# Differential attention of a two-block transformer: the values product issued one unit later than the transposes

## What is computed

```python
def diff_attention(q, k, v, lam):
    s = jnp.einsum('bqhpd,bkhpd->bhpqk', q, k).astype(jnp.float32) * (ATT_HEAD_DIM ** -0.5)
    p = jax.nn.softmax(s, axis=-1)
    a = p[:, :, 0] - lam * p[:, :, 1]
    return jnp.einsum('bhqk,bkhe->bqhe', a.astype(v.dtype), v)
```

## Time and profile before

| what | us |
|---|---|
| median of three runs | 3123.93 |
| lowest and highest | 3122.47, 3125.21 |
| the profiled execution, its device time | 3122.81 |
| span of its trace | 3121.0 |
| TensorE busy | 2692.0 (86%) |
| VectorE busy | 1351.0 (43%) |
| ScalarE busy | 483.3 (15%) |
| chain that ended last: loads of expert weights (`in_moe_w`) | 12% of the span |
| attention stage of layer 0, first S to the end of the last o | 206.69 to 255.26 |
| attention stage of layer 1, likewise | 910.53 to 944.03 |

### The profile page before, as it was taken

One profiled execution on the slowest core, in us unless ns is written; L12 is line 12 of the kernel. 1 busy time (PEld: TensorE's weight loads), 2 busy tenths in 40 slices (PEclk: granted clock), 3 DMA queues, 4 the chain that ended last, 5 costly groups with the idle time before them and its releaser, 6 DMA issues. The chain is left out here.

```text
span 3121.0 us, 45633 instructions
## 1 busy us (share of the span) xinstructions
PE 2692.0 (86%) x19942; PEld 1662.7 (53%) x19942; DVE 1351.0 (43%) x2546; ACT 483.3 (15%) x1169; POOL 39.9 (1%) x64
## 2 busy tenths in 40 slices
PE   6988999999988999987969989879979787756656
PEld 3457844446766888635543334345459686422323
DVE  1874488533472876686221101121466763100001
ACT  1023200000122001234221001010051301100000
POOL 0000000000000000001000000000000000000000
PEclk8999999999999999998979999989999898878877
DMA  8530255432342675220229999981110016799998
GB/s 341 193 135 1 92 204 216 151 145 111 130 164 73 269 287 208 81 81 1 82 107 427 427 428 427 428 337 30 43 35 29 2 72 231 299 427 427 427 428 350
DMA packets 66358, 651.35 MB, mean 209 GB/s; under 512 B 14704, under 2 KB 25584, under 8 KB 26480
## 3 DMA queue, kind: packets, MB, share of 16 engines
q1 hardware_dynamic: 66160, 648.43, 51.5%
HBM read 644.08 MB, written 4.33 MB: 208 GB/s over the span
## 5 line engine op out<-in xcount | busy, mean ns | idle before, releaser
L369 PE MATMUL ps<-HT,ring 128*128 128x256 f32 (+1 forms) x3024 | 902.7, 458 | 29.3 <-DMA ring<-in_w_in 10.9
L369 PEld LDWEIGHTS ps<-HT,ring 128*128 128x128 f32 x3024 | 573.0, 191 | 333.7 <-issue 271.0
L1952 PE MATMUL ps<-ring,arena 128*32 128x256 f32 (+1 forms) x2976 | 374.1, 506 | 105.9 <-DMA ring<-in_moe_w 103.2
L442 DVE SCALAR_TENSOR_TENSOR acc<-ring,sil,acc 128x512 f32<-128x512 f32 x616 | 411.7, 744 | 0.0
L369 PE MATMUL ps<-arena,ring 128*128 128x256 f32 (+3 forms) x1232 | 373.6, 464 | 3.2 <-PEq L644 2.0
L1952 PEld LDWEIGHTS ps<-ring,arena 128*32 128x32 f32 (+1 forms) x2976 | 141.4, 130 | 316.0 <-issue 200.3
L369 PEld LDWEIGHTS ps<-arena,ring 128*128 128x128 f32 (+2 forms) x1232 | 230.1, 188 | 139.2 <-issue 119.1
L948 DVE SCALAR_TENSOR_TENSOR XT<-ps,modcols,XT 128x256 f32<-128x256 f32 x148 | 66.6, 481 | 356.0 <-PE ps L369 228.3
L1973 PE MATMUL ps<-ring,conv 128*64 128x512 f32 x512 | 116.1, 596 | 27.7 <-DMA ring<-in_moe_w 26.9
L1973 PE MATMUL ps<-ring,arena 128*32 128x256 f32 x960 | 86.0, 520 | 61.5 <-DMA ring<-in_moe_w 61.0
L369 PE MATMUL ps<-ring,HT 128*128 128x512 f32 (+1 forms) x288 | 105.1, 523 | 0.0
(11 more groups left out here) (366 smaller groups left out, 2657.4 us busy)
## 6 DMA issues: line engine op xcount, KB each, us to landing
ring<-in_moe_w SPq DMA_DIRECT2D x186, 2048.0 KB, 25.6
ring<-in_w_mod SPq DMA_DIRECT2D x24, 2048.0 KB, 8.4
ring<-in_ada_w SPq DMA_DIRECT2D x24, 2048.0 KB, 8.3
ring<-in_w_up SPq DMA_DIRECT2D x16, 2048.0 KB, 12.3
ring<-in_w_down SPq DMA_DIRECT2D x16, 2048.0 KB, 12.6
ring<-in_w_in SPq DMA_DIRECT2D x10, 2048.0 KB, 10.3
ring<-in_od_w_in SPq DMA_DIRECT2D x6, 2048.0 KB, 25.6
arena<-in_moe_w SPq DMA_DIRECT2D x10, 1024.0 KB, 7.3
```

The costliest lines, as they stand in the source:

```text
L369: last = nc.tensor.matmul(bank_of(job, j), lhsT, rhs, start=n == 0, stop=n == len(terms) - 1)
L442: ins = nc.vector.scalar_tensor_tensor(out=acc, in0=weights[:, k, :], scalar=s, in1=acc, op0=ALU.mult, op1=ALU.add)
L1952: last = nc.tensor.matmul(K.ps[M * j:M * j + M, 2 * (e % 2) + i, 0:FW], xs[:, e // 4 % 2, e % 4, 4 * h + k, :], weights((m, e, h), k, slic ...
```

## The change

On TensorE each turn now issues T(i-3), S(i), V(i-4); on ScalarE c(i-3), e(i); on VectorE o(i-5), m(i), p(i-1). VectorE's wait for e(i-4) ahead of m(i) is gone. The loops have one turn more. The instructions themselves, their operands, their number and the buffers stay as they are. Nothing outside this function changes.

```diff
         @block.tensor
         def _(pe):
-            for i in range(U + 3):
+            for i in range(U + 4):
+                if 3 <= i <= U + 2:
+                    j = i - 3
+                    pe.wait_ge(*K.at("probs_done", 2 * (j + 1)))
+                    if j:
+                        pe.wait_ge(*K.at("probsT_done", j))
+                    for c in range(len(units[j]["v"])):
+                        last = nc.tensor.matmul(K.ps[:, 6, c * P:(c + 1) * P], E[:, j % nb, 0, c * P:(c + 1) * P], scaled_ident[:, j % 4],
+                                                start=True, stop=True)
+                    last.then_inc(*K.inc("transposed"))
                 if i < U:
...
-                if i >= 3:
-                    j = i - 3
+                if i >= 4:
+                    j = i - 4
                     u = units[j]
                     pe.wait_ge(*K.at("probsT_done", j + 1))
...
-                if 2 <= i <= U + 1:
-                    j = i - 2
-                    pe.wait_ge(*K.at("probs_done", 2 * (j + 1)))
...
-                    last.then_inc(*K.inc("transposed"))
         @block.scalar
         def _(act):
-            for i in range(U + 2):
+            for i in range(U + 3):
+                if i >= 3:
+                    j = i - 3
+                    act.wait_ge(*K.at("transposed", j + 1))
+                    if j >= 2:
+                        act.wait_ge(*K.at("values_done", j - 1))
+                    n = P * len(units[j]["v"])
+                    nc.scalar.activation(AT[:, j % 2].rearrange("p k q -> p (k q)")[:, 0:n], K.ps[:, 6, 0:n], ACT.Copy).then_inc(*K.inc("probsT_done"))
                 if i < U:
...
-                if i >= 2:
-                    j = i - 2
-                    act.wait_ge(*K.at("transposed", j + 1))
...
         @block.vector
         def _(dve):
-            for i in range(U + 4):
-                if i >= 4:
-                    j = i - 4
+            for i in range(U + 5):
+                if i >= 5:
+                    j = i - 5
                     dve.wait_ge(*K.at("values_done", j + 1))
                     nc.vector.tensor_copy(units[j]["out"], K.ps[:, 7, 0:P]).then_inc(*K.inc("out_kept"))
                 if i < U:
                     n = units[i]["k"].shape[-1]
                     dve.wait_ge(*K.at("scores_done", i + 1))
-                    if i >= 4:
-                        dve.wait_ge(*K.at("exps_done", 2 * (i - 3)))
```

## The result

The changed kernel takes 3119.53 us (median of 22 runs, 3115.42 to 3123.84) against 3123.69 us before (22 runs, 3118.36 to 3129.64). The ratio is 0.9985, 95% interval 0.9979 to 0.9991: by it the change is worth 4.7 us, between 2.8 and 6.6 (the two medians are 4.2 apart). That is less than the 0.2% that was called no change, and it lies clear of zero. Forecast were 5.2 us and 3118.7.

What follows compares the result with a forecast made beforehand. The prediction took the two-unit chain S, m, e, c, V, T, with V waiting for c, to bound the wide units. Layer 0's 3.07 us and layer 1's 2.12 sum to 5.2 saved, giving 3118.7 us, range 3115.0 to 3123.5.

Steps and rivals of the forecast that it cites:

- The new bound of wide units: Wide units, steady state: TensorE alone, S to V to T to S, 3.04 us per unit in place of 3.23.
- The chain that bounds a head of layer 0: Layer 0, S9 to S11 over m, p, o, V6 and T8: 5.55 us of a 10.32 us head.
- the gain is passed on: After both attention stages: what they save is saved in full; the rival, not passed on, 3123.9 us, chance 0.08.
- The hand-over from o to V: VectorE to TensorE: o itself 0.28 us and 0.05 to hand over, 0.33 together.
- the tail of layer 0: Layer 0, S15 to the end of the last o: 7.96 us after, 8.24 before, 0.28 less.
- The tail of layer 1: Layer 1, S7 to the end of the last o: 10.99 us after, 11.45 before, 0.46 less.
- Layer 1: Second attention stage: start 0.89, S4 to S7 0.77 and tail 0.46, together 2.12 us saved.
- the chain through ScalarE: Wide units: S, m, e, c, V, T closes over three units, 6.46 / 3 = 2.15 us each, and drops out.
- the first rival: Layer 0: TensorE alone bounds it, a head takes 9.54 us; 7.3 us saved, 3116.6 us; chance 0.16.
- The wait for o: Slower rival: V(i-4) waits on `out_kept`, two-unit chain 7.31 us if o comes behind one p more; about 3132 us; chance 0.03.
- the 0.3 per head that was named as a sign: Layer 0: V's idle wait for o, expected at about 0.3 us per head if the forecast holds.
- The clock rival: Low-clock stretch on TensorE more or less, 1.7 us either way: 3117.0 or 3120.4 us; chance 0.13.

Runs made afterwards that it cites:

- the one kernel above that does not fit: Changed kernel with V(i-5), o(i-6) and room for three units in AT: 3119.45 us, ratio 0.9981 to the kernel before.
- the first pair of traces: First traced execution of the kernel before and of the changed kernel: layer 0 48.54 and 46.09 us, layer 1 33.47 and 30.80.
- the second traces on both sides: Kernel before and changed kernel traced again without edit: layer 0 48.54 and 47.15 us, layer 1 31.53 and 29.74.
- the two repeats: Changed kernel run twice more without edit: 3120.19 and 3120.55 us, ratios 0.9990 and 0.9991 to the kernel before.

## Why the prediction was right, and where not

**What held.** Order, not work: T keeps its place among the S's, ScalarE's list is unchanged, and only V moves; the kernel with V and o alone moved shows it. The new bound of wide units, 3.04 us of TensorE, was met to the hundredth. The chain that bounds a head of layer 0, S9, m, p, o, V, T, S11, is the one in the trace: 229.11 to 234.74 is 5.63 us, forecast 5.55. That the gain is passed on holds by the traces; by the medians it holds for most of it, with the one kernel above that does not fit.

**The mis-sized term.** The hand-over from o to V was put at 0.33 us, 0.28 for o and 0.05 taken over from c to V. Where V stood idle for o, the trace has 0.43 from the start of o to V's matmuls (232.81 to 233.24). That is 0.10 more in each link from p to V, and 0.08 from one V to the next (1.61 for 1.53), where the end of V came sooner. In the tail of layer 0, with four such links, it is all that was missing: 7.96 forecast, 253.42 - 245.14 = 8.28 measured, before 8.24. So the tail gained nothing where 0.28 was forecast. From S4 to S15, with three such links, layer 0 took 29.03 us, forecast 28.79, and its start gave 0.84 for 0.89. In all it saved 48.54 - 46.09 = 2.45 us, forecast 3.07.

**A hit by two errors.** The tail of layer 1 was forecast at 10.99 and took 10.88. S7 to V4 took 4.12 us for 4.02, again by o. But the four steps V4, T6, V5, T7, V6 took 3.77 for 3.96: T to V had been priced with the 1.09 of T to S. The prediction's 0.89 and 1.09 also count T from its weight load, which stands 0.11 ahead of its matmuls; together they are right, taken one by one they are not comparable with times between matmuls.

**Layer 1** saved 2.67 us in the first pair of traces, forecast 2.12, but that pair holds two pieces of luck: the clock in S0 to S4 and the phase of S4 to S7. With the second traces on both sides, where S0 to S3 took 6.52 us before and after, it is 31.53 - 29.74 = 1.79: 0.84 by the start (forecast 0.89), 0.39 from S4 to S7 (forecast 0.77, read where two steps of three were long ones) and 0.57 by the tail (forecast 0.46). The means of two traces before and three after give 32.50 - 30.45 = 2.05. In layer 0 the same means give 48.54 - 46.44 = 2.10. Together 4.15 us, beside 4.7 measured (3.1 and 2.8 in the two repeats, all three intervals clear of zero) and 5.2 forecast. That the forecast lies within 0.5 us of the measured 4.7 is in part luck: the three measured values differ by more than that.

**A step that was wrong and cost nothing.** The prediction let the chain through ScalarE close over three units and drop out. It doesn't: T(i-2) also waits for c(i-3), so S, m, e, c, T, S still closes over two units, without V's 0.89: 6.46 - 0.89 = 5.57 us for wide ones. That is under TensorE's 6.08, and in layer 0 it hid just under the chain through o. The kernel with o on ScalarE laid it open (S9 to S11 5.42 us, beside 5.63 through o), and the one with c ahead of e removed it. For the same reason the first rival, TensorE alone in layer 0, could not come true by a faster o alone.

**The other rivals.** The wait for o did come up: 0.66 us on one V of a head and 0.20 on another, beside the 0.3 per head that was named as a sign; the chain through it came out 0.08 us over its sum, far from the 0.46 from which the stage would be slower than before. The clock rival is real in size: 0.9 us at the start of layer 0 in one trace of the changed kernel out of three, and up to 1.6 in layer 1. Low stretches come at the starts, behind an idle TensorE, in executions of both kernels, which is where the rule of the Trainium skill (TensorE: Matmul & The Clock Gate, Part 1: The HAM clock gate), throttled unless activity releases it, puts them. The traces agree as to the place; behind the same 3.01 us of idle time at the start of layer 0 seven traces show 1.00 and six the low level. The 1.7 us that the prediction let it give the changed kernel can't be told from this scatter.

## What to carry to other kernels

Before moving a stage in a pipeline written out by hand, write out the resulting order of each engine: a turn of the loop is no time, and half of this diff was the same program in other words. A wait is worth the difference to the next chain that closes, so list every wait of every instruction on it, the one for the freed bank too, before you call a chain gone. When two chains lie close together, here 5.63 us through o and 5.42 through c, removing one gives only the difference (0.2 us in a head of 10.4). The next gain takes both at once: with o on ScalarE, which is busy for 15% of the span, and c ahead of e, the stages got shorter by 4.0 us, nearly as much again as by the change itself.

## What the runs showed of the hardware that was not expected

- The granted clock behind the same 3 us pause of TensorE was 1.00 in one execution and 0.53 in another of the same kernel, and moved S3 to S4 from 2.27 to 3.19 us. In this program it went with the moment at which the stage began; the latest start with the low clock and the earliest with the high one were 0.08 us apart. A single trace of a short stage carries about 1 us of that.
- Two copies of 128x128 one behind the other on VectorE start 0.20 us apart, though each is shown with 0.28, while TensorE starts 0.43 us after the last one's start. The recorded durations gave neither interval here; start to start did.
